# A two-block transformer on one core: the second mixer's head roots, table sets and first logits are placed anew

## What is computed

```python
qx = apply_rope(rmsnorm(heads(px[0], 8, 64), g_q), cos, sin)     # 8 query heads
kx = apply_rope(rmsnorm(heads(px[1], 2, 64), g_k), cos, sin)     # 2 key heads, 512 tokens
kc = rmsnorm(heads(pc[1], 2, 64), g_k)                           # 256 context keys, not rotated
att_x = latent_attention(qx, concat(kc, kx), concat(vc, vx))     # softmax over 768 keys
# a gated linear recurrence in both directions, 4 heads of 128:
#   q = silu(.), f = lb + (1-lb)*sigmoid(.), k = 1 - f, states by log f and exp
o = rmsnorm(o_f + o_b, gain);  hg_x = o * silu(gate)
x = x + m2 * (concat(att_x, hg_x) @ w_out)
```

## Time and profile before

| | us |
|---|---|
| median of 3 runs (2129.98 to 2130.57) | 2130.34 |
| the profiled execution | 2127.93 |
| its span, first to last instruction | 2126.2 |
| PE busy (share of the span) | 2028.2 (95%) |
| DVE busy | 1235.8 (58%) |
| ACT busy | 902.3 (42%) |
| POOL busy | 368.2 (17%) |
| second mixer's loop, first logits to next stage's first product | 1604.1 to 1696.1 |

### The profile page before, as it was taken

One profiled execution on the slowest core, in us unless ns is written; L12 is line 12 of the kernel. 1 busy time (PEld: TensorE's weight loads), 2 busy tenths in 40 slices (PEclk: granted clock), 3 DMA queues, 4 the chain that ended last, 5 costly groups with the idle time before them and its releaser, 6 DMA issues. The chain is left out here.

```text
span 2126.2 us, 27406 instructions
## 1 busy us (share of the span) xinstructions
PE 2028.2 (95%) x9738; PEld 1623.1 (76%) x9738; DVE 1235.8 (58%) x1894; ACT 902.3 (42%) x1387; POOL 368.2 (17%) x412
## 2 busy tenths in 40 slices
PE   8899999999999999999999998899997989999997
PEld 6666666888888678778888875888875778888886
DVE  3666547888677646766655334678756553333333
ACT  4433735444422444354443226666557543222222
POOL 0033501000000101000000001677635700000000
PEclk9999999999999999999999999999998999999999
DMA  5511013566444322222333221111110022233321
GB/s 175 152 48 40 1 50 110 178 191 193 149 161 161 110 82 90 79 76 93 98 99 115 95 76 60 41 41 40 58 52 1 21 80 85 94 98 99 111 102 44
DMA packets 52782, 193.97 MB, mean 91 GB/s; under 512 B 5809, under 2 KB 8529, under 8 KB 52313
## 3 DMA queue, kind: packets, MB, share of 16 engines
q1 hardware_dynamic: 44824, 165.18, 24.4%
q0 software_dynamic: 7344, 27.27, 4.1%
q10 hardware_dynamic: 528, 0.40, 0.1%
HBM read 189.15 MB, written 3.68 MB: 91 GB/s over the span
## 5 line engine op out<-in xcount | busy, mean ns | idle before, releaser
L196 PE MATMUL psum<-xH,w_hi 128*128 128x512 f32 x1800 | 726.2, 403 | 41.1 <-DVE xL L1377 20.4
L196 PE MATMUL psum<-xL,w_hi 128*128 128x512 f32 x1800 | 708.8, 394 | 0.0
L196 PE MATMUL psum<-xH,w_lo 128*128 128x512 f32 x1800 | 708.7, 394 | 0.0
L166 DVE TENSOR_TENSOR w_lo<-w_raw,w_hi 128x1024 fp32r<-128x1024 f32 (+1 forms) x273 | 355.1, 1301 | 329.0 <-ACT w_hi L160 328.7
L160 ACT ACTIVATE w_hi<-w_raw 128x1024 fp32r<-128x1024 f32 (+1 forms) x273 | 303.2, 1111 | 418.4 <-PE psum L196 409.0
L196 PEld LDWEIGHTS psum<-xH,w_hi 128*128 128x128 f32 x1800 | 342.6, 190 | 139.2 <-DVE xL L1377 36.2
L196 PEld LDWEIGHTS psum<-xH,w_lo 128*128 128x128 f32 x1800 | 342.5, 190 | 73.6
L196 PEld LDWEIGHTS psum<-xL,w_hi 128*128 128x128 f32 x1800 | 343.2, 191 | 71.0 <-issue 3.4
L196 PE MATMUL psum<-hidH,w_hi 128*128 128x512 f32 x528 | 206.2, 391 | 0.0
L196 PE MATMUL psum<-hidH,w_lo 128*128 128x512 f32 x528 | 205.4, 389 | 0.0
L196 PE MATMUL psum<-hidL,w_hi 128*128 128x512 f32 x528 | 205.4, 389 | 0.0
(11 more groups left out here) (321 smaller groups left out, 2504.8 us busy)
## 6 DMA issues: line engine op xcount, KB each, us to landing
w_raw<-in_up SPq DMA_DIRECT2D x132, 512.0 KB, 3.5
w_raw<-in_down SPq DMA_DIRECT2D x48, 704.0 KB, 4.0
mod_raw<-in_mod POOLq DMA_DIRECT2D x48, 512.0 KB, 3.9
w_raw<-in_sb_in SPq DMA_DIRECT2D x26, 512.0 KB, 3.6
w_raw<-in_ev_in SPq DMA_DIRECT2D x23, 512.0 KB, 3.6
w_raw<-in_od_in SPq DMA_DIRECT2D x20, 512.0 KB, 3.5
w_raw<-in_ev_out SPq DMA_DIRECT2D x8, 512.0 KB, 3.5
w_raw<-in_od_out SPq DMA_DIRECT2D x8, 512.0 KB, 3.5
```

The costliest lines, as they stand in the source:

```text
L166: nc.vector.tensor_tensor(w_lo[:, s % SPLIT, 0:w.cols], raw[:, s, 0:w.cols], w_hi[:, s % SPLIT, 0:w.cols].bitcast(F32), ALU.subtract).then ...
L196: mm = nc.tensor.matmul(acc, a[:, slot % SPLIT, cut], b[:, k0 + k, :], start=start and n == 0, stop=stop and n == 2)
```

## The change

- `load_log_exp` places a load of the set that has both Ln and Exp. It stands after the query gates of heads 2 and 3, after the sigmoids of heads 1 to 3, after every `gate_logs`, before the first softmax exponential, and after the last chunk's result.
- `head_mean`'s copy on ACT and the block `head_rstd` go. `head_root(n)` does Ln straight from bank 2 and then Exp, at the part where the copy was.
- DVE scales the heads at parts 70 to 72 instead of after the parts.
- ACT makes the high keys at part 72, the first high queries and Silu of gates 0 and 1 at part 73; gates 2 and 3 are taken out of PSUM by Silu in place of Copy.
- PE computes `logits(0)` between the halves of the last chunk, behind the recurrence's last `output`. The logits of even steps go to banks 2 and 3, of odd steps to banks 0 and 1, the other way round than before. ACT does `exponential(0)` ahead of the last chunk's result.
- `o_rstd` of the last recurrence head moves behind step 3's exponential, its use on DVE (`head_out`) to step 5.

```diff
+        def load_log_exp():
+
+            nc.scalar.preload_act_table_set("natural_log_exp_and_others")
...
+        LAST_ROOT, LAST_Y = 3, 5
...
+        SCALED = {70: (0, 1), 71: (2, 3, 4), 72: (5,)}
...
-            return slice((u % 2) * 1024 + 256, (u % 2) * 1024 + 1024)
+            c0 = (1 - u % 2) * 1024
+            return slice(c0 + 256, c0 + 1024)
...
-                                                      ACT.Silu if name == "hq" else ACT.Copy), c)
+                                                      ACT.Silu if name == "hq" or name == "hg" and m >= 2 else ACT.Copy), c)
+                    if name == "hq" and c >= RAW or c == w.n - 1:
+                        load_log_exp()
                     self.high(act, 0, c, c + SPLIT < w.n)
...
                     for u in (2 * hd, 2 * hd + 1):
                         for f in (bx(u), bc(u)):
                             nc.scalar.activation(f, f, ACT.Sigmoid).then_inc(g["sig"], 1)
+                    if hd:
+                        load_log_exp()
...
                     act.wait_ge(g["k"], 4 * hd + 4)
                     for u in (2 * hd, 2 * hd + 1):
                         for f in (bx(u), bc(u)):
                             nc.scalar.activation(f, f, ACT.Ln).then_inc(g["ln"], 1)
+                    load_log_exp()

...
-                    hd = due(n, 24, 2 * LEVELS, HG)
+                    hd = due(n, 24, 2 * LEVELS, HG - 1)
                     if hd is not None:
...
-                def head_mean(n):
+                def head_root(n):
                     act.wait_ge(b["mean"], n + 1)
-                    nc.scalar.activation(nrs[n], bank[2][:, 0:width(n)], ACT.Copy).then_inc(b["rstd"], 1)
-
-                def head_rstd():
-                    for n in range(NT):
-                        act.wait_ge(b["rstd"], n + 1)
-                        nc.scalar.activation(nrs[n], nrs[n], ACT.Ln, bias=cols[:, e:e + 1]).then_inc(b["rstd"], 1)
-                    for n in range(NT):
-                        act.wait_ge(b["rstd"], NT + n + 1)
-                        nc.scalar.activation(nrs[n], nrs[n], ACT.Exp, scale=-0.5).then_inc(b["rstd"], 1)
+                    nc.scalar.activation(nrs[n], bank[2][:, 0:width(n)], ACT.Ln, bias=cols[:, e:e + 1]).then_inc(b["rstd"], 1)
+                    act.wait_ge(b["rstd"], 2 * n + 1)
+                    nc.scalar.activation(nrs[n], nrs[n], ACT.Exp, scale=-0.5).then_inc(b["rstd"], 1)
+
+                def keys_high():
+                    act.wait_ge(b["scaled"], 2)
+                    for kv in range(2):
+                        for far in range(2):
+                            nc.scalar.activation(kst[rows(kv ^ far), kv, 0, :], kall[rows(kv), :], ACT.Copy).then_inc(b["k_hi"], 1)
+
+                def queries_high(i, kv):
+                    nc.scalar.activation(qst[kv][rows(kv), :, blk(i)], query_rows(kv, i), ACT.Copy).then_inc(b["q_hi"], 1)
+
+                def first_gates():
+                    for m in range(2):
+                        self.there(act, SB_LIST.index(("hg", m)))
+                    first = sb_hT[:, HG_TILE:HG_TILE + 2, :]
+                    nc.scalar.activation(first, first, ACT.Silu).then_inc(hg_in, 1)
+
+                def exponential(u):
+                    act.wait_ge(b["max"], u + 1)
+                    if u >= 4:
+                        act.wait_ge(b["prob_t"], turns(u - 4))
+                    nc.scalar.activation(pr2[:, u % 4, :], wide[:, logit_cols(u)], ACT.Exp, bias=st2[:, 0, u:u + 1],
+                                         accum_out=st2[:, 1, u:u + 1]).then_inc(b["exp"], 1)

                 result(0)
...
-                        head_mean(MEANS[p - 1])
+                        head_root(MEANS[p - 1])
                     if p == 72:
-                        head_rstd()
+                        keys_high()
+                    if p == 73:
+                        act.wait_ge(b["scaled"], NT)
+                        for kv in range(2):
+                            queries_high(0, kv)
+                        first_gates()
+                load_log_exp()
+                exponential(0)
                 result(w.n - 1)
-
-                def queries_high(i, kv):
-                    nc.scalar.activation(qst[kv][rows(kv), :, blk(i)], query_rows(kv, i), ACT.Copy).then_inc(b["q_hi"], 1)

                 def prob_out(u):
...
-                act.wait_ge(b["scaled"], NT)
-                for kv in range(2):
-                    for far in range(2):
-                        nc.scalar.activation(kst[rows(kv ^ far), kv, 0, :], kall[rows(kv), :], ACT.Copy).then_inc(b["k_hi"], 1)
-                    queries_high(0, kv)
-                for m in range(HG):
...
-                    if u < U2:
-                        act.wait_ge(b["max"], u + 1)
-                        if u >= 4:
-                            act.wait_ge(b["prob_t"], turns(u - 4))
-                        nc.scalar.activation(pr2[:, u % 4, :], wide[:, logit_cols(u)], ACT.Exp, bias=st2[:, 0, u:u + 1],
-                                             accum_out=st2[:, 1, u:u + 1]).then_inc(b["exp"], 1)
+                    if 0 < u < U2:
+                        exponential(u)
+                    if u == LAST_ROOT:
+                        o_rstd(HG - 1)
                     if u in (U2 + 2, U2 + 3):
                         split_high(act, w.next, 0, u - U2 - 2)
                     hd = due(u, 9, 2, HG)
...
-                    hd = due(n, 26, 2 * LEVELS, HG)
+                    hd = due(n, 26, 2 * LEVELS, HG - 1)
                     if hd is not None:
-                        dve.wait_ge(g["rstd"], 2 * hd + 2)
-                        nc.vector.scalar_tensor_tensor(hq(hd), hq(hd), gain_hg[:, :], ors, ALU.mult, ALU.mult).then_inc(g["y"], 1)
+                        head_out(hd)
+
+                def head_out(hd):
+                    dve.wait_ge(g["rstd"], 2 * hd + 2)
+                    nc.vector.scalar_tensor_tensor(hq(hd), hq(hd), gain_hg[:, :], ors, ALU.mult, ALU.mult).then_inc(g["y"], 1)

                 def head_gain(v):
                     n = turned(v)
...
-                for n in range(NT):
-                    dve.wait_ge(b["rstd"], 2 * NT + n + 1)
-                    if n == 1:
-                        nc.vector.scalar_tensor_tensor(kall[:, 0:LC], head_tile(n), gain_of(n), nrs[n], ALU.mult, ALU.mult)\
-                            .then_inc(b["scaled"], 1)
-                    else:
-                        dve.wait_ge(b["roped"], n if n else 1)
-                        nc.vector.tensor_tensor(kall[:, LC:NK] if n == 0 else head_tile(n), head_tile(n), nrs[n], ALU.mult)\
-                            .then_inc(b["scaled"], 1)
+                    for n in SCALED.get(p, ()):
+                        dve.wait_ge(b["rstd"], 2 * n + 2)
+                        if n == 1:
+                            nc.vector.scalar_tensor_tensor(kall[:, 0:LC], head_tile(n), gain_of(n), nrs[n], ALU.mult, ALU.mult)\
+                                .then_inc(b["scaled"], 1)
+                        else:
+                            dve.wait_ge(b["roped"], n if n else 1)
+                            nc.vector.tensor_tensor(kall[:, LC:NK] if n == 0 else head_tile(n), head_tile(n), nrs[n], ALU.mult)\
+                                .then_inc(b["scaled"], 1)

                 def queries_low(i, kv):
...
+                    if u == LAST_Y:
+                        head_out(HG - 1)
                     if u < U2 and u % 8 == 4 and u // 8 + 1 < NB:
...
                         dve.wait_ge(hg_in, 1)
+                        if hd >= 2:
+                            self.there(dve, SB_LIST.index(("hg", hd)))
...
                 def head_turn(v):
                     pe.wait_ge(b["gain"], v + 1)
-                    pe.wait_ge(b["rstd"], v + 2)
+                    pe.wait_ge(b["rstd"], 2 * v + 3)
                     nc.tensor.matmul(bank[2][:, :], turn64[:, :], head_tile(turned(v)), start=True, stop=True).then_inc(b["rot"], 1)
+
+                def logits(u):
+                    i, r, kv = u // 8, (u // 2) % 4, u % 2
+                    if u >= 2:
+                        pe.wait_ge(b["exp"], u - 1)
+                    elif u == 0:
+                        pe.wait_ge(b["sin"], NR)
...
+                    else:
+                        self.there(pe, w.n - 2)
+                        self.there(pe, w.n - 1)
...
+                    if r == 0:
+                        pe.wait_ge(b["q_lo"], 2 * i + kv + 1)
+                    q = qst[kv][:, r, blk(i)]
+                    c0 = (1 - u % 2) * 1024
+                    for c, k in ((256, slice(0, LC)), (512, slice(LC, NK))):
...
+                        mm = nc.tensor.matmul(wide[:, c0 + c:c0 + c + k.stop - k.start], q, kst[:, kv, 1, k], start=False, stop=True)
+                    mm.then_inc(b["logits"], 1)
...
                 for p, (c, ctx, k0) in enumerate(PARTS):
                     part(c, ctx, k0)
                     gla(job(p - PE_AT))
```

(49 more changed lines are left out.)

## The result

The changed kernel takes 2117.36 us (median, 2117.0 to 2118.96), the kernel before beside it 2130.32: a ratio of 0.9941, interval 0.9928 to 0.9953, 12.96 us. Two more comparisons gave 2116.94 (ratio 0.9934, 0.992 to 0.9948) and 2116.99 (0.9935, 0.9922 to 0.9949). The forecast was 2116.9, the range 2113.5 to 2123.0. The profiled execution's own time is 2117.15 us around a span of 2115.5, 10.8 less than before's 2127.93.

What follows compares the result with a forecast made beforehand. TensorE is busy nearly all the span, so only its standstills count: 4.1 us at the first rotation plus 9.3 us from last chunk to loop, 13.4 us off the median 2130.34, gives 2116.9 us, range 2113.5 to 2123.0.

Steps and rivals of the forecast that it cites:

- A: First rotation: second head's mean read sooner without loads, 2.5 us, and no low clock behind it, 1.6 us; together 4.1 us.
- Rival 3: At every root: placed loads don't hold, Ln and Exp still switch sets; 2126.3 us, chance 0.08.
- perhaps 0.15 us later: DVE work queued behind the heads' scalings at parts 70 to 72 comes that much later; nothing subtracted, 0.5 us kept in range.
- my signs of being wrong: Wrong if PE idles before logits(0), a load separates Ln and Exp, a wait precedes the last chunk, or the loop lengthens.
- B: From last chunk to attention loop: first values earlier by 9.5 us at full clock, taken as 9.3, bounds 6 and 10.8.
- the ladder: Step-by-step times from last chunk to loop: exp(1) 10.0 us, exp(3) 10.8 us, values(0) 9.8 us earlier.
- the clock's term: Between 1601.7 and 1612, PE half busy: low clock would make values(0) 9.0 us earlier; 9.3 taken, against 9.5 at full clock.
- Rival 4: Attention loop: low clock holds on into dense steps, up to 2.2 us each; ten steps give 2139 us; chance 0.04.
- Hidden early logits: logits(0) inside the last chunk: operands ready 4.8 us early, no wait; costs 0.78 us itself, new loads 1.3 us before PE.
- The loop shifts as a block: Attention loop from values(0) to its end: starts and ends earlier by the same time, length unchanged within 1 us.
- the rest of the span as fixed: Everything outside the first rotation and the stretch from last chunk to loop: only a fixed shift, no gain or loss.
- rival 1: Smaller shift at both places: clock falls or other operand late at first rotation, later hops lost; 9.5 us, 2120.8, chance 0.22.

Runs made afterwards that it cites:

- both edits: Changed kernel with the heads' scaling on DVE one step later and logits(0) behind the last chunk again: 2115.18 us, 0.9929.
- all three: Changed kernel with later heads' scaling, logits(0) behind the last chunk, and last o_rstd behind step 5's exponential: 2114.38 us, again 2114.57 us.
- the logits alone: Changed kernel with logits(0) behind the last chunk again and result(25) ahead of the first softmax exponential: 2116.62 us, 0.9933.
- the scaling alone: Changed kernel with the heads' scaling on DVE one step later, at parts 72 and 73: 2114.35 us, 0.9926.

## Why the prediction was right, and where not

The result is within 0.5 us of the forecast, but part of that is two errors that cancel, so the steps count more than the sum.

- **A, 4.1 us: right, measured 4.21**, and 4.32 with the sets alone. ACT's four instructions came as laid out, the Ln of 256 columns at 0.46 us where I took 0.48; the wait was 1.45 where I had 1.6, and the granted clock stayed at 1.00. Rival 3 (the placed loads don't hold) fell with it; the run without the set showed what it would have been, but dearer than I had it: the first rotation itself came 1.5 us later than before where I had 1.4, but its stretch ended 2.1 us later, and the median is 2129.08 where I had 2126.3.
- **The scalings "perhaps 0.15 us later": mis-sized, 1.25 us.** The transposes for the values are 2.96 us earlier behind the mark (44.80 against 47.76) where A alone would make it 4.21. PE's wait in front of chunk 25 grew from 0.57 to 1.73 us, and a wait in front of the last chunk was one of my signs of being wrong. I had counted what is queued on DVE at its durations alone. The price of the keys' scaling in company, 1.78 us, was not in a row of mine, but POOL's instruction of that kind taking 2.20 us where its median is 1.29 stood in the trace of before, beside the DVE instruction L166.
- **B, 9.3 us: the ladder right, the clock's term mis-sized; 8.0 measured.** Counted from the values' transposes (1588.76 in the plan's times), plan and trace are: `logits(0)` 8.29 and 8.33, exp(0) 10.94 and 11.01, `logits(1)` 13.94 and 14.01, exp(1) 15.94 and 15.98, exp(3) 18.84 and 19.03, exp(5) 24.14 and 24.31. Then the first `values`, 26.74 at a granted clock of 1.00 and 28.50 measured. In the timeline of PE shown above a step's logits take 1.43 us here (1611.68 to 1613.11) and 0.78 at 1.00, the transposes behind them 1.41 against 0.75: 1.3 us of the 1.8. I had put the low clock early, where PE idles anyway, at 0.5 us or so; it came late, when PE had no idle time left. The runs where it stayed away reach the first `values` in 26.0 and 26.4 us, and the one where it fell earlier, with the root back, in 26.7. Rival 4 took this fall and made it last thirty; it lasted about 4 (0.90, 0.50, 0.75 and 1.00 in the four windows of 2 us from 1610).
- **Hidden early logits: no gain.** The wait I added up for `logits(0)` cost nothing, as forecast, but what it buys does not pay either: without it the two loads of 1.3 us that I named in front of `logits(1)` are one.
- **The loop shifts as a block: right.** From the second `values` to the next stage 66.45 us before, 66.14 after, 66.1 to 67.1 in all runs but the one with the root back (68.67), in which the clock fell a second time inside the loop.
- **Outside the change: missed.** I took the rest of the span as fixed. The next norm gains 1.4 us, since the load between its Ln and Exp is gone; and the clock's fall at the stage's start takes 1.6 back where it happens.
- **The sum.** In the mixer 11.05 us came of 13.4, which is nearer to rival 1 (9.5) than to the forecast, though by neither of rival 1's reasons: no hop of the ladder was lost, and A was whole. With the norm and the clock the profiled executions differ by 10.8; the medians by 13.0 to 14.1. The profiled execution of before lies 2.4 us below its median, that of after 0.2 below its own; only one profile of before is kept, so where its other executions spend those 2.4 us isn't known. Applied to the profiled execution my 13.4 us gave 2114.5, which was 2.65 too low; applied to the median, 2116.9. That agreement is partly luck: the mixer fell 2.35 us short of the forecast, and the 2.4 us by which before's median lies over its profile made up for it.

**Open.** Why the clock fell at the next stage's start (at 1686.7, to 0.50) in all three profiled executions of the changed kernel, with the root put back, with both edits and with all three, and not in those of before, of the joint set alone, without the joint set, of the logits alone and of the scaling alone: it comes behind the same 1.84 us of idle time in before and after, and I tried nothing on it. How often it falls in executions without a profile isn't known either, and neither is why the low clock at 1612 came in some of these kernels and not in others, nor why it came inside the loop with the root back. So what the move of the last root brings by itself is open too. Differences of 1 to 2 us between the medians here can be the clock's as well as the edit's; the markers in front of those places are what the verdicts rest on.

## What to carry over

Where two functions alternate in front of a waiting engine, look first for a table set that has both and pin it where the code loads another: it gave nearly two thirds of this change, and the moved work brought 1.7 us by medians without it. Before work is moved into an engine's gap, look who else is active in that gap: the keys' scaling, 0.69 us before, took 1.78 beside POOL's rotation. And where one engine of a loop has no gaps, an earlier start ahead of it finds it busy: exp(4) 1.3 us earlier brought nothing at the loop's end, so an edit should be priced there and not at its first steps. Before a lost lead is put down to a wait, look at the granted clock where it is lost: with the root back, 1.6 us went there.

## What the hardware showed that I had not expected

- DVE and POOL beside each other: the keys' scaling of 0.69 us took 1.78, and POOL's rotation, about 1.28 us in three of five before, took 2.20. The times fit the three running one after the other: L166 ends at 1578.90, POOL's at 1580.05, the keys' scaling at 1580.60. With the scaling moved away POOL's instruction still takes 2.21 us, so it isn't the scaling that holds it up; L166 is beside it in both. That they take turns is read out of these rows, not tested by itself.
- ACT has 54 loads before, 43 in the changed kernel and 66 without the joint set, 1.28 us each. Without the set, the Ln and the Exp of each of the six head roots have a load of their own; in the changed kernel none of them has one.
- A placed load was carried out even where the same load stood before it, as behind `gate_logs`: behind the one at 1374.31 Exp (1375.61) and Ln (1379.70) run with no load ahead of them, and the one at 1381.47 takes 1.28 us again. The trace has all eleven placed loads, 1.28 us each. The nine in the projection brought no wait of PE: besides the one for the head, PE waits for ACT 2.7 and 2.3 us in 1310 to 1600, before the change and after. The last two stand in front of the 1.14 us ahead of `logits(1)`.
- The granted clock fell at 1611.7, near the end of 14 us of work with gaps (PE busy 8.67 of 14 us in 1598 to 1612), and was 1.00 again in 1616 to 1618. In the version with all edits, PE's share in 1600 to 1608 was 5.27 of 8 us and the clock stayed at 1.00; in the changed kernel it was 5.85 of 8 and the fall came all the same.
